# Sparse-attention stacks planned head by head, top-k steps and latent sums moved, in a two-block fp32 transformer kernel

## The chip, the cores and the metric

The kernel runs on one core of one Trainium2 chip. The metric is the device time of one execution in microseconds (us), lower is better. PE is the matrix engine (TensorE), DVE the vector engine, ACT the scalar engine, POOL GpSimd, and SP the engine whose queue issues all DMAs here.

## The reference

`first_block` (pooling, gated linear attention, forgetting attention, gated feed-forward) is followed by `second_block`, both on a [512, 1024] fp32 activation. The change touches the second block only:

```
h = rmsnorm(x, norm_g)
q_lat, c_kv, k_rope, z_a, q_b, k_b, v_b, z_b, q_idx, k_idx, w_idx, gate_a, gate_b = split(h @ w_in)
q  = rmsnorm(q_lat, g_q_lat) @ w_uq          # 8 heads of 64 + 32 (rope)
kv = rmsnorm(c_kv, g_kv_lat) @ w_ukv         # latent ("mla") attention
y_a = mla_attention(q, kv, rope(k_rope)) * silu(z_a)          # 8 heads, chunk-causal
score = sum over 8 index heads of relu(q_idx . k_idx) * w_idx  # per query block of 128
idx = top_k(score, 128)                       # keys a query may see
y_b = dsa_attention(q_b, k_b, v_b, idx, rel_bias) * silu(z_b)  # 8 heads of 64
x = x + (sigmoid(gate_a) * (y_a @ w_o_a) + sigmoid(gate_b) * (y_b @ w_o_b)) @ w_out
```

## The kernel before

Activations lie transposed, [feature, token], so a product is a chain of 128x128 weight tiles against 128x512 activations. Each fp32 product is done as three matmuls on rounded halves (WH with the high and low half of the activation, WL with the high half: L1346, L1347, L1348). Weights come as 164 units of eight tiles through three buffers (WS); ACT rounds a unit (WH, L1516), POOL or DVE subtracts (WL, L2090 or L1765), and SP loads the unit three further on when the subtraction is done.

A planner in Python writes one list of steps; each engine then runs its own instructions of that list in that order, each waiting on semaphores. So an instruction that waits holds all that stand behind it on its engine. A product of n tiles is planned in pieces of two tiles (six matmuls). `weave(main, side, per)` plans one turn of the main generator (index scores, or attention, two turns for each block of 128 queries of a head) and then `per` pieces of the side generator. At every piece but the last of a product, `go_behind` adds `now["per"]` to a due count and plans as many steps from the lists `first` (DSA stacks) and then `behind` (top-k) as are due.

The second block, in order:

- Index scores: for query blocks i = 3, 2, 1 and eight heads, one matmul (L1496), a relu on ACT (L1710), and a weighted sum on DVE into `score` (L2007, L2010). Four banks and four relu buffers rotate. When a block's scores are summed, its cut (L2014) and 16 top-k steps follow, each a MAX8 (L2019) and a MATCH_REPLACE8 (L2021) on 128 x 128(i+1) values, then the mask (L2026). The side work is `latents`: the products ckv0, ckv1, ql0, ql1, ql2 and za0. Each output goes through DVE (L2030), a square on ACT (L1524), a sum on POOL (L2135, L2138), and is halved by ACT (L1714) and DVE (L2035). The column sums (L1377, L1383) of the squares of ckv feed `norm_kv` on ACT (L1718 to L1726: Ln, Ln, Exp, Exp with two table loads), those of ql feed `norm_q` (L1729, L1732). `mla_v` and the first `mla_products` follow. Outputs of query products (a_q) leave their bank on DVE (L2046).
- Attention: four pairs of latent heads, then four pairs of DSA heads, woven with `mla_side`: the other latent products, the DSA products qb, kb and v, the z gates, and the output gates and products. Four a_q, a_k buffers rotate.
- A DSA head needs a stack in one of three slots: the high and low half of q in `b_s1`, the high half of k twice in `b_m1`, the low half twice in `b_m2`. ACT rounds q and k (L1692, L1694), DVE subtracts (L1979, L1982), and SP copies each k half to the other 64 partitions (L1274, L1279). The logits are L1455 and L1456. A head's slot is free again when its last logits are done. `st` (b_st) holds a pair's products until its stacks are made. Before, the stacks of a pair are planned as five steps; a pair's attention begins (`dsa_ready`) when all five are planned, the masks are planned, and the pair's gate zb is there.
- RT holds the rotation table, read for the rope of the keys and by `norm_q` (L2039).

Of the kernel before, what the change touches and what calls it, by code (L numbers as in the profile page):

```python
# [9 lines left out]
F32R = mybir.dt.float32r  # L10
# [152 lines left out]
def build(nc, wall, xT, vecs, wa, wp, relb, cf, cph, coh, cb, scratch, outT):  # L163
    plan = []
    ctx = ExitStack()
    with ctx:
# [104 lines left out]
        LKL = sub("LKL", [128, 2, T], F32R, 32)  # L271
        sq0, sq1 = (at(f"sq{i}_late", [128, T], F32R, o) for i, o in enumerate(sq_at))
        b_s1 = [sub("b_s10", [128, T], F32R, 16), sub("b_s11", [128, T], F32R, 22), sub("b_s12", [128, T], F32R, 56)]
        b_m1 = [sub("b_m10", [128, T], F32R, 18), sq1, sub("b_m12", [128, T], F32R, 64)]
        b_m2 = [sub("b_m20", [128, T], F32R, 20), sub("b_m21", [128, T], F32R, 2), sq0]
        b_st = [[sqb[0], sub("b_st0", [128, T], F32, 2)], [sub("b_st1", [128, T], F32, 58), sub("b_st2", [128, T], F32, 52)],
                [sub("b_st3", [128, T], F32, 58), sub("b_st4", [128, T], F32, 66)]]
# [630 lines left out]
        do("keys", t1=t1, free1=free1, t2=t2, free2=free2)  # L908
        tmp_ring.give(m1, rope("end"))
        tmp_ring.give(m2, rope("end"))  # L910
        now["per"] = 0.6

        def index_scores():
            for i in (3, 2, 1):
# [29 lines left out]
        def latents():  # L944
            for c in range(2):
                yield from product(f"ckv{c}", "w_in_2", 0, cols(P_CKV + 128 * c), "h3", NK,
                                   lat_out(c, "lk", f"ckv{c}", acc[1]))
            bias_rows()
            do("row_out")
            for c in range(3):  # L950
                yield from product(f"ql{c}", "w_in_2", 0, cols(P_QL + 128 * c), "h3", NK,
                                   lat_out(c, "lq", f"ql{c}", acc[0]))
                do("copy_rows", heads=((0, 1, 2), (3, 4, 5), (6, 7))[c])
                if c == 0:
                    i1, b1 = column_sums("lk", acc[1], total_g(("lk", 1)))
                    i2, b2 = token_sums("lkt", [acc[1]], total_g(("lk", 1)))
                    do("norm_kv", b1=b1, b2=b2)
                    t_ring.give(i1, norm_a("lk ln"))
                    t_ring.give(i2, norm_a("lkt ln"))
            for n, _ in enumerate(z_products("za", P_ZA, 0)):  # L960
                if n == 2:
                    i, b = column_sums("lq", acc[0], total_g(("lq", 2)))
                    do("norm_q", b=b)
                    t_ring.give(i, norm_a("lq ln"))
                yield
# [82 lines left out]
        slot_ring, bt_ring = Ring([0, 1, 2]), Ring(b_t)  # L1048
        pc_ring = Ring(Pc)
        pc_ring.free = [None, None, idx_v((1, 7))]  # L1050
        dsa_in, slot_of = {}, {}
        bias_at = {}

        def dsa_v():
# [12 lines left out]

        def dsa_stack(p):

            for n in range(5):  # L1070
                hl, what = n // 2, "qk"[n % 2]
                if n < 4:
                    if what == "q":
                        while not slot_ring.ready() or "uq7" not in known:
                            yield "not yet"
                        i, _, free = slot_ring.take()
                        slot_of[2 * p + hl] = i, free
                    i, free = slot_of[2 * p + hl]
                    do("bstack_high", p=p, hl=hl, what=what, i=i, free=free)
                if n > 0:  # L1080
                    hl, what = (n - 1) // 2, "qk"[(n - 1) % 2]
                    i, free = slot_of[2 * p + hl]
                    do("bstack_low", p=p, hl=hl, what=what, i=i, free=free)
                if n == 4:
                    dsa_in[p] = True
                yield

        def dsa_products(p):
            while (p == 1 and ("logits", ("mla", 5, 3)) not in known) or (p == 2 and ("logits", ("mla", 7, 3)) not in known) \
                    or (p >= 2 and p - 1 not in dsa_in):  # L1090
                go_behind()
                yield "not yet"
            free = [[total_g(("lq", 2)), idx_p((1, 7))], [logits(("mla", 5, 3))], [logits(("mla", 7, 3))], []][p]
# [6 lines left out]

        def dsa_pair(p):
            z_i, z = gates[f"zb{p}"]

            def begun(hl, i, u):
                hd = 2 * p + hl
                if i == 3:
                    bt_ring.give(bias_at[hd][0], row_max(u))
                    slot_ring.give(slot_of[hd][0], logits(u))
                if i == 0:
                    dsa_bias(hd + 1)  # L1110
            return {"a": "dsa", "p_no": p, "qk": [slot_of[2 * p][0], slot_of[2 * p + 1][0]], "begun": begun, "to": "yb",
                    "to_n": p, "z": z, "z_ring": z_ring, "z_i": z_i, "bias": bias_at}

        def gate(m, kind, col, g):
# [24 lines left out]
        def mla_side():  # L1139
# [2 lines left out]
            yield from mla_products(2)  # L1142
            yield from gate_a(0)
            yield from mla_products(3)
            yield from dsa_v()
            dsa_bias(0)
            yield from z_products("zb", P_ZB, 0)
            yield from dsa_products(1)
            yield from gated_ya(0)
            yield from z_products("zb", P_ZB, 1)  # L1150
            yield from dsa_products(2)
            yield from z_products("zb", P_ZB, 2)
            yield from gate_a(1)
            yield from dsa_products(3)
            yield from gated_ya(1)
            yield from z_products("zb", P_ZB, 3)
            for m in range(2, 8):
                yield from gate_a(m)
                yield from gated_ya(m)

        def dsa_ready(p):
            if p not in dsa_in or "masks" not in known:
                step_behind()
            return p in dsa_in and "masks" in known and f"zb{p}" in gates

        now["per"] = 1.4
        side = mla_side()
        for _ in range(3):
            next(side)
# [1120 lines left out]
```

## Time and profile before

| | |
|---|---|
| median of 3 runs | 1110.09 us (1109.54 to 1114.36) |
| the profiled execution, its own time | 1110.54 us |
| its span, first to last instruction | 1108.8 us |
| PE busy | 1052.4 us (95%) |
| DVE, ACT, POOL busy | 625.8 (56%), 474.4 (43%), 261.7 (24%) us |
| mean granted TensorE clock | 0.984 |

Busy time is the time in which an engine runs an instruction. "PEclk" is the TensorE clock that was granted, as a share of the full 2.4 GHz. In lists of instructions a bracket at the end gives how long the engine stood idle ahead of the instruction and what released it. Where a wait has several conditions, the one named is an inference.

### The profile page before, as it was taken

What the parts mean: (1) busy time and instruction counts of PE and PEld (TensorE: products, weight loads), DVE (VectorE), ACT (ScalarE), POOL (GpSimd) and SP (SyncE); (2) the same over time, 40 slices, a digit from 0 to 9 for tenths busy, and PEclk for the clock granted to TensorE, in tenths of its full rate; (3) what the DMA queues carried; (4) which work ended last, traced back from release to release, by engine and by line L of the source; (5) the groups of instructions that cost most, each with busy time, mean ns of one, the idle gap of its engine ahead of it and who ended that gap; (6) DMA issues with size and microseconds to landing.
All of it is one profiled execution on the core that took longest, in us unless ns stands there. A gap on an engine that the chain in (4) does not pass through costs nothing.

```text
span 1108.8 us, 13432 instructions
## 1 busy us (share of the span) xinstructions
PE 1052.4 (95%) x5124; PEld 843.6 (76%) x5132; DVE 625.8 (56%) x1038; ACT 474.4 (43%) x819; POOL 261.7 (24%) x158
## 2 busy tenths in 40 slices
PE   7799899899999999999999998899999999999995
PEld 5597687677888888888888776677887766788883
DVE  6755667756445432444445366898656664325554
ACT  6634345545323221222243456455655453423232
POOL 0581332222110100001113333222322322421101
PEclk9899999999999999999999999999999999999998
DMA  7031132212322232232323326211322333222221
GB/s 291 9 125 42 58 97 89 67 57 79 111 96 95 95 114 95 77 109 85 111 95 96 107 69 201 77 58 58 96 67 91 93 98 90 77 95 93 98 95 76
DMA packets 33919, 103.37 MB, mean 93 GB/s; under 512 B 4576, under 2 KB 6000, under 8 KB 33856
## 3 DMA queue, kind: packets, MB, share of 16 engines
q1 hardware_dynamic: 33856, 102.51, 28.3%
q8 instruction: 41, 0.67, 0.3%
q14 instruction: 22, 0.18, 0.1%
HBM read 94.40 MB, written 4.74 MB: 89 GB/s over the span
## 4 chain that ended last, share of the span: by engine, by line
PE 75%; DVE 13%; ACT 5%; issue 4%; SPq 2%; DMA 1%; DVEq 0%; ACTq 0%; POOL 0%; POOLq 0%
PE bank L1346 21%; PE bank L1348 20%; PE bank L1347 20%; PE bank L1478 2%; PE bank L1469 2%; PE bank L1358 2%; PE bank L1360 1%; PE bank L1359 1%; DVE score L2010 1%; DVE m L2019 1%; DVE score L2021 1%; ACT WH L1516 1%; DVE f_s L1809 1%; PE bank L1450 1%; DVE acc L1779 1%
## 5 line engine op out<-in xcount | busy, mean ns | idle before, releaser
L1346 PE MATMUL bank<-HH,WH 128*128 128x512 f32 x808 | 330.3, 409 | 15.9 <-DVE WL L1765 8.1
L1348 PE MATMUL bank<-HH,WL 128*128 128x512 f32 x808 | 318.3, 394 | 0.0
L1347 PE MATMUL bank<-HL,WH 128*128 128x512 f32 x808 | 317.6, 393 | 0.0
L2090 POOL TENSOR_TENSOR WL<-WS,WH 128x1024 fp32r<-128x1024 f32 x64 | 154.9, 2421 | 360.1 <-ACT WH L1516 359.7
L1516 ACT ACTIVATE WH<-WS 128x1024 fp32r<-128x1024 f32 x164 | 170.7, 1047 | 56.0 <-PE bank L1348 40.6
L1346 PEld LDWEIGHTS bank<-HH,WH 128*128 128x128 f32 x808 | 154.3, 191 | 52.8 <-DVE WL L1765 8.1
L1348 PEld LDWEIGHTS bank<-HH,WL 128*128 128x128 f32 x808 | 153.2, 190 | 33.5
L1347 PEld LDWEIGHTS bank<-HL,WH 128*128 128x128 f32 x808 | 153.9, 191 | 29.5 <-issue 1.0
L1765 DVE TENSOR_TENSOR WL<-WS,WH 128x1024 fp32r<-128x1024 f32 x100 | 132.7, 1333 | 29.5 <-ACT WH L1516 29.5
L2143 POOL TENSOR_TENSOR fa<-fa,fg 128x512 f32<-128x512 f32 x22 | 28.3, 1286 | 273.4 <-DVE fa L1956 273.4
L1346 PE MATMUL bank<-GH,WH 128*128 128x512 f32 x176 | 68.5, 389 | 0.0
L1347 PE MATMUL bank<-GL,WH 128*128 128x512 f32 x176 | 68.5, 389 | 0.0
L1348 PE MATMUL bank<-GH,WL 128*128 128x512 f32 x176 | 68.5, 389 | 0.0
L1936 DVE TENSOR_TENSOR X<-X,bank 128x512 f32<-128x512 f32 x40 | 27.4, 685 | 65.0 <-PE bank L1348 64.9
L1659 ACT ACTIVATE GH<-fa 128x512 fp32r<-128x512 f32 x22 | 13.9, 632 | 114.3 <-POOL fa L2143 114.3
L1524 ACT ACTIVATE sq<-X 128x512 f32<-128x512 f32 x31 | 19.5, 628 | 71.6 <-DVE X L1936 71.5
L1358 PE MATMUL bank<-WH,HH 128*128 128x256 f32 x160 | 47.8, 299 | 2.0 <-ACT f_v L1542 2.0
L1627 ACT ACTIVATE PT<-bank 128x128 f32<-128x128 f32 (+1 forms) x96 | 41.2, 429 | 17.9 <-PE bank L1469 17.6
L1360 PE MATMUL bank<-WH,HL 128*128 128x256 f32 x160 | 45.7, 286 | 0.0
L1359 PE MATMUL bank<-WL,HH 128*128 128x256 f32 x160 | 45.7, 285 | 0.0
L1958 DVE TENSOR_TENSOR GL<-fa,GH 128x512 fp32r<-128x512 f32 x22 | 15.2, 693 | 46.8 <-ACT GH L1659 46.8
L1655 ACT ACTIVATE fs<-fg 128x512 f32<-128x512 f32 x22 | 13.9, 632 | 59.6 <-DVE fg L1947 59.6
(336 smaller groups left out, 1748.5 us busy)
## 6 DMA issues: line engine op xcount, KB each, us to landing
WS<-wall SPq DMA_DIRECT2D x164, 512.0 KB, 3.4
scratch<-rows SPq DMA_DIRECT2D x8, 320.0 KB, 5.4
X<-xT SPq DMA_DIRECT2D x8, 256.0 KB, 6.9
b_t<-scratch SPq DMA_DIRECT2D x8, 256.0 KB, 3.8
b_m<-b_m SPq DMA_DIRECT2D x11, 128.0 KB, 4.3
outT<-X SPq DMA_DIRECT2D x5, 256.0 KB, 2.3
f_s<-f_s SPq DMA_DIRECT2D x8, 128.0 KB
f_m<-f_m SPq DMA_DIRECT2D x8, 128.0 KB
```

The costliest lines, as they stand in the source:

```text
L1346: e.matmul(b[:, :], wh, xh[:, at_k, :], start=k == 0, stop=False)
L1347: e.matmul(b[:, :], wh, xl[:, at_k, :], start=False, stop=False)
L1348: m = e.matmul(b[:, :], wl, xh[:, at_k, :], start=False, stop=k == n - 1)
L1358: e.matmul(b[:, 0:256], xh[:, k, cs], wh, start=k == 0, stop=False)
L1359: e.matmul(b[:, 0:256], xh[:, k, cs], wl, start=False, stop=False)
L1360: m = e.matmul(b[:, 0:256], xl[:, k, cs], wh, start=False, stop=k == NK - 1)
L1516: e.activation(WH[:, u % NW, :], WS[:, u % NST, :], ACT.Copy).then_inc(*w_hi.tick(u))
L1627: e.activation(dst, s["b"][:, 0:128 * i + 128].rearrange("p (a n) -> p a n", n=128), ACT.Copy).then_inc(*moved.tick(s["u"]))
L1765: e.tensor_tensor(WL[:, u % NW, :], WS[:, u % NST, :], f32(WH[:, u % NW, :]), ALU.subtract).then_inc(*w_low_v.tick(u))
L1936: e.tensor_tensor(X[:, m, :], X[:, m, :], s["b"][:, :], ALU.add).then_inc(*out_v.tick(s["name"]))
L2090: e.tensor_tensor(WL[:, u % NW, :], WS[:, u % NST, :], f32(WH[:, u % NW, :]), ALU.subtract).then_inc(*tick(w_low_g, u))
L2143: e.tensor_tensor(a[:, :], a[:, :], fg[jj % 3][:, :], ALU.mult).then_inc(*tick(gate_up, jj))
```

## The change

Five edits, all in the planner; the instructions of each engine stay the same in kind and number, and their order changes.

1. `b_m12`, the k high half of slot 2, moves from the place at 64 KB (which a latent head's a_q buffer shares) to the memory of RT.
2. Top-k steps: `per` 0.6 becomes 0.4 in the index scores, and 1.4 becomes 1.45 in attention.
3. The column and token sums of the ckv squares, with norm_kv, move from behind ql0 to behind ql1.
4. A DSA stack is planned for each head by itself, three steps each, and a pair may begin when its first head's stack is planned; the second head's is asked for at the first head's last query block.
5. `mla_side` has another order: gate_a(1), dsa_products(1) and zb0 go ahead of dsa_v, zb1 ahead of gated_ya(0), gated_ya(1) ahead of dsa_products(3).

```diff
-        b_m1 = [sub("b_m10", [128, T], F32R, 18), sq1, sub("b_m12", [128, T], F32R, 64)]
+        b_m1 = [sub("b_m10", [128, T], F32R, 18), sq1, at("b_m12", [128, T], F32R, RT_at)]
...
-        now["per"] = 0.6
+        now["per"] = 0.4
...
-                if c == 0:
+                if c == 1:
                     i1, b1 = column_sums("lk", acc[1], total_g(("lk", 1)))
                     i2, b2 = token_sums("lkt", [acc[1]], total_g(("lk", 1)))
                     do("norm_kv", b1=b1, b2=b2)
...
         def dsa_stack(p):
-            for n in range(5):
-                hl, what = n // 2, "qk"[n % 2]
-                if n < 4:
-                    if what == "q":
-                        while not slot_ring.ready() or "uq7" not in known:
-                            yield "not yet"
-                        i, _, free = slot_ring.take()
-                        slot_of[2 * p + hl] = i, free
-                    i, free = slot_of[2 * p + hl]
-                    do("bstack_high", p=p, hl=hl, what=what, i=i, free=free)
-                if n > 0:
-                    hl, what = (n - 1) // 2, "qk"[(n - 1) % 2]
-                    i, free = slot_of[2 * p + hl]
-                    do("bstack_low", p=p, hl=hl, what=what, i=i, free=free)
-                if n == 4:
-                    dsa_in[p] = True
-                yield
+            for hl in range(2):
+                hd = 2 * p + hl
+                while not slot_ring.ready() or "uq7" not in known:
+                    yield "not yet"
+                i, _, free = slot_ring.take()
+                for n in range(3):
+                    if n < 2:
+                        do("bstack_high", p=p, hl=hl, what="qk"[n], i=i, free=free)
+                    if n > 0:
+                        do("bstack_low", p=p, hl=hl, what="qk"[n - 1], i=i, free=free)
+                    if n == 2:
+                        slot_of[hd] = i
+                    yield
...
-                    or (p >= 2 and p - 1 not in dsa_in):
+                    or (p >= 2 and 2 * p - 1 not in slot_of):
...
         def dsa_pair(p):
             z_i, z = gates[f"zb{p}"]
+            qk = [slot_of[2 * p]]
...
-                    slot_ring.give(slot_of[hd][0], logits(u))
+                    slot_ring.give(slot_of[hd], logits(u))
+                    if hl == 0:
+                        while hd + 1 not in slot_of:
+                            step_behind()
+                        qk.append(slot_of[hd + 1])
...
             yield from mla_products(3)
+            dsa_bias(0)
+            yield from gate_a(1)
+            yield from dsa_products(1)
+            yield from z_products("zb", P_ZB, 0)
             yield from dsa_v()
-            dsa_bias(0)
-            yield from z_products("zb", P_ZB, 0)
-            yield from dsa_products(1)
+            yield from z_products("zb", P_ZB, 1)
             yield from gated_ya(0)
-            yield from z_products("zb", P_ZB, 1)
             yield from dsa_products(2)
             yield from z_products("zb", P_ZB, 2)
-            yield from gate_a(1)
+            yield from gated_ya(1)
             yield from dsa_products(3)
-            yield from gated_ya(1)
             yield from z_products("zb", P_ZB, 3)
...
         def dsa_ready(p):
-            if p not in dsa_in or "masks" not in known:
+            if 2 * p not in slot_of or "masks" not in known:
                 step_behind()
-            return p in dsa_in and "masks" in known and f"zb{p}" in gates
-
-        now["per"] = 1.4
+            return 2 * p in slot_of and "masks" in known and f"zb{p}" in gates
+
+        now["per"] = 1.45
```

## Rows read from the trace of the kernel before

**Rows 1.** The page, busy us, share of the span and instructions.
```profile
PE 1052.4 (95%) x5124; PEld 843.6 (76%) x5132; DVE 625.8 (56%) x1038; ACT 474.4 (43%) x819; POOL 261.7 (24%) x158
```

**Rows 2.** Windows: PE, PEld, DVE, ACT, POOL busy (count), granted clock, DMA share, GB/s.
```profile
500.00:600.00 100.00, 100.00 (x443) 82.84 (x442) 48.68 (x53) 33.71 (x44) 18.43 (x15) 1.00 0.29 95
...
660.00:716.00 56.00, 46.11 (x211) 36.60 (x210) 43.03 (x57) 30.29 (x51) 20.39 (x10) 0.93 0.45 145
716.00:755.00 39.00, 37.93 (x178) 27.94 (x177) 34.17 (x84) 18.58 (x46) 9.58 (x4) 0.96 0.17 54
...
885.00:930.00 45.00, 40.34 (x196) 30.86 (x197) 28.53 (x76) 20.53 (x47) 12.14 (x6) 0.96 0.38 109
```

**Rows 3.** PE's waits from 660 to the end: us in total, times, longest.
```profile
PE bank L1377 <- POOL acc L2138: 4.4, 1, 4.4
PE bank L1346 <- DVE a_q L2046: 4.3, 2, 3.1
```

**Rows 4.** Timeline of PE, logits of heads 4, 6: start, us, [idle, releaser].
```profile
890.11 0.30 PE L1455 MATMUL bank<-sq_late,b_s 128*128 128x128 f32 x1 [1.99 <-DVE sq_late L1982]
...
923.35 0.30 PE L1455 MATMUL bank<-b_m,b_s 128*128 128x128 f32 x1 [2.48 <-issue]
```

**Rows 5.** Timeline of PE, index scores and latents.
```profile
681.20 0.34 PE L1496 MATMUL bank<-i_kk,i_qq 96*128 96x384 f32 x1
...
688.85 2.08 PE L1377 MATMUL bank<-acc,ones 128*128 128x512 f32 x2 [4.36 <-POOL acc L2138]
...
713.95 0.50 PE L1346 MATMUL bank<-LQH,WH 128*128 128x512 f32 x1 [3.07 <-DVE a_q L2046]
```

**Rows 6.** Windows of 8 us around three of PE's waits.
```profile
688.00:696.00 8.00, 7.15 (x23) 5.38 (x23) 7.77 (x10) 6.73 (x10) 3.42 (x2) 0.57 0.20 75
712.00:720.00 8.00, 6.05 (x22) 4.83 (x23) 6.92 (x17) 0.86 (x3) 0.00 (x0) 0.79 0.20 66
920.00:928.00 8.00, 5.52 (x21) 4.18 (x20) 2.40 (x9) 2.56 (x5) 2.43 (x1) 0.79 0.63 178
```

**Rows 7.** Timeline of ACT around norm_kv and behind ql1.
```profile
666.88 1.28 ACT L1718 ACT_TABLE_LOAD   x1
668.18 0.69 ACT L1718 ACTIVATE RK<-bank,eps 128x512 f32<-128x512 f32 x1
...
671.25 1.06 ACT L1516 ACTIVATE WH<-WS 128x1024 fp32r<-128x1024 f32 x1 [0.19 <-DMA WS<-wall]
...
679.37 1.05 ACT L1516 ACTIVATE WH<-WS 128x1024 fp32r<-128x1024 f32 x1
```

**Rows 8.** Timeline of DVE, two score lines.
```profile
681.11 2.37 DVE L2007 TENSOR_SCALAR score<-i_t,wi 128x384 f32<-128x384 f32 x1
...
709.09 2.42 DVE L2010 SCALAR_TENSOR_TENSOR score<-i_t,wi,score 128x256 f32<-128x256 f32 x1
```

**Rows 9.** Timeline of POOL, the subtraction beside the first of them.
```profile
680.56 2.70 POOL L2090 TENSOR_TENSOR WL<-WS,WH 128x1024 fp32r<-128x1024 f32 x1 [0.77 <-ACT WH L1516]
```

**Rows 10.** Timeline of DVE, one top-k step on 512 columns.
```profile
711.43 0.68 DVE L2019 MAX8 m<-score 128x8 f32<-128x512 f32 x1
...
712.23 0.68 DVE L2021 MATCH_REPLACE8 score<-m,score 128x512 f32<-128x512 f32 x1
```

**Rows 11.** Timeline of DVE, outputs of kb2 and kb3, low halves of k.
```profile
875.07 0.69 DVE L1782 SCALAR_TENSOR_TENSOR b_st<-bank,Rb 128x512 f32<-128x512 f32 x1 [1.94 <-PE bank L1348]
...
880.89 0.67 DVE L1982 TENSOR_TENSOR b_m<-b_st,sq_late 64x512 fp32r<-64x512 f32 x1
...
909.32 0.68 DVE L1782 SCALAR_TENSOR_TENSOR b_st<-bank,Rb 128x512 f32<-128x512 f32 x1
...
916.00 1.98 DVE L1982 TENSOR_TENSOR b_m<-b_st,b_m 64x512 fp32r<-64x512 f32 x1
```

**Rows 12.** Timeline of SP's queue, copy of head 4's low half of k.
```profile
885.50 0.47 SPq L1279 DMA_DIRECT2D b_m<-b_m  x1
```

**Rows 13.** The tile b_m, time from issue to landing of its copies.
```profile
DMA to landing us min/median/max: 2.2/4.3/4.9
```

More of the change, by code:

```diff
@@ L1050, in build @@
         pc_ring.free = [None, None, idx_v((1, 7))]
-        dsa_in, slot_of = {}, {}
+        slot_of = {}
         bias_at = {}
@@ L1107, in begun @@
                     bt_ring.give(bias_at[hd][0], row_max(u))
-                    slot_ring.give(slot_of[hd][0], logits(u))
+                    slot_ring.give(slot_of[hd], logits(u))
[3 more added lines that the diff above has]
+                        qk.append(slot_of[hd + 1])
                 if i == 0:
                     dsa_bias(hd + 1)
-            return {"a": "dsa", "p_no": p, "qk": [slot_of[2 * p][0], slot_of[2 * p + 1][0]], "begun": begun, "to": "yb",
+            return {"a": "dsa", "p_no": p, "qk": qk, "begun": begun, "to": "yb",
                     "to_n": p, "z": z, "z_ring": z_ring, "z_i": z_i, "bias": bias_at}
```

## The prediction

> **What bounds the kernel now.** First the busy times of the page [rows 1]: the matrix engine (PE) is busy for 95% of the span and no other engine passes 56%, so only time in which PE stands still, or runs at its lower clock, can be won or lost by a change that adds no matmul. The long feed-forward stretch [rows 2] shows the undisturbed rate: 443 matmuls in 100 us, 0.226 us each. Then the same view for the stretches of the second block: PE misses 9.9 us of the 56 between 660 and 716 (latents and index scores) and 4.7 of the 45 between 885 and 930 (DSA attention); between 716 and 755 it misses 1.1 [rows 2]. The list of PE's waits names them [rows 3]: 4.4 us for the sum of squares of the query latents and 4.3 for two query outputs (a_q); 2.0 and 2.5 at two DSA logits (L1455) stand in [rows 4]. The clock column adds what follows a wait [rows 5, 6]: in the 8 us around the wait that ends at 688.85 the granted clock is 0.57 (8 times 0.43, 3.4 us lost), around the one that ends at 713.95 it is 0.79 (1.7), and around the one that ends at 923.35 [rows 4] 0.79 again (1.7); 0.50 of it is the lower of the two levels, 1.2 of 2.4 GHz. So 13.2 us of waits and 6.8 us of low clock are all there is to win; no rate of top-k steps gives more.
>
> **Part 1: the latent sums and norm_kv go from behind ql0 to behind ql1.** Nothing is added: 1 column sum and 4 token sums on PE, six instructions on ACT. What counts is where ACT meets them. In the trace they run from 666.88 on, two table loads of 1.28 us among them, and the weight copy behind them starts at 671.25 after 0.19 us of idling for its DMA [rows 7]: 4.2 us of work, all of it done before the copy could start. The weight load came late because the index and key copies stood ahead of it on SP's queue, and the change moves none of these. So ahead of ql1 the 4.2 us are hidden, and taking them away lets no later relu start sooner. Behind ql1 they fall between the relu of (3,7) and the weight copy that now starts at 679.37 [rows 7], where ACT has no slack: copy and the relus of (2,0) to (2,2) go from 679.4 to 683.6. The engine (DVE) that sums the scores then starts (2,0) at 685.1 instead of 681.1, and is held by POOL's subtraction as it is now: POOL 680.56 for 2.70 us, the DVE line 681.11 for 2.37 [rows 8, 9]; both move by 4.2. The latent of ql2, queued behind (2,0), (2,1), (2,2), comes 4.2 us later, less the one top-k step (1.44, below) that no longer stands ahead of it: +2.8. PE waits on it through square, POOL sum and column sum: 688.85 becomes 691.6 [rows 5]. A new wait comes ahead of it: the index matmul (2,4) needs the bank that the relu of (2,0) empties, so PE, which starts it at 681.20 now [rows 5], stands until 685.1.
>
> On the price of the table loads the trace and the Trainium skill differ. In [rows 7] the load takes 1.28 us and the Ln behind it begins at once. The Trainium skill (ScalarE: Activation LUTs, What ACT_TABLE_LOAD costs) gives about 2.66 us for a switch, its drain included; by that the moved group would take 6.9 us and this part would cost 2.8 us more. The measured group decides.
>
> **Part 2: top-k steps, 0.6 to 0.4 for each piece, then 1.4 to 1.45.** A piece is a pair of k tiles (six matmuls, 1.36 us); a step is planned at a piece that is not the last of its product. Counting through the seven such pieces between the first mask cut and the end of the scores gives 4 steps now and 2 after, and the two that go are the ones ahead of the last two a_q outputs. A step on 512 columns is a MAX8 and a MATCH_REPLACE8 of 0.68 us each with a short load between them, 1.44 us [rows 10]. PE stood 1.2 and 3.07 us for these outputs [rows 3, 5]. With everything 2.95 us later by part 1 and two steps (2.9) fewer, the last output would come when it does now; but the score ahead of it, held for 2.42 us [rows 8] by POOL, then comes before POOL's next subtraction, whose weight copy follows PE. PE gets on at 712.6 instead of 713.95: -1.35 (0 if the score is held all the same). Of the 1.7 us at low clock behind that wait I take half as won, since the new waits of 3.9 us (part 1) and near 2.9 (the first output that mla_v needs, zb at L1782) can leave a slow phase of their own: -0.85. The two steps are paid back later: 44 steps become 46, and by piece 22 of latent attention 1.1 steps more have run than now (1.5 us). DVE is busy 34.2 of 39 us there and PE has 1.1 us idle [rows 2], so most is hidden: +0.5, bounds 0 and 1.4. If the whole delay of part 1 stayed and the cover were gone, parts 1 and 2 would cost +4.2; at best they give -3.0. Sum: -1.7.
>
> **Part 3: order of the side work, stacks by head, b_m12 in RT.** The memory only removes a clash: head 2's stack can be written while latent head 7 still uses the old place. RT is last read by norm_q, long before. No instruction is added; a stack has three steps a head (six a pair, five now). dsa_products(1) and gate_a(1) go ahead of dsa_v, so heads 2 and 3 are ready early, but nothing waits for them now: PE's only waits at L1455 are at heads 4 and 6 [rows 4]. So heads 4 and 6 decide. A pair starts when its zb gate is known and its first stack is planned. I count pieces at 0.9 and 0.85 for each half unit of attention, with the not-ready turns (the count gives the one turn seen ahead of pair 0). From the last piece of kb2 to the first logit of head 4: 7 pieces and 4 units now, 5 pieces and 2 units after, because dsa_products(2) moves behind zb1 and gated_ya(0) and pair 2 starts on zb2. From kb3 to head 6: 7 pieces now, 5 after, since gated_ya(1) goes ahead of dsa_products(3). In time: kb2 leaves at 875.07 and PE reaches head 4 at 888.1, 13.0 us; kb3 at 909.32, head 6 at 920.9, 11.6 us [rows 4, 11]. Less two pieces (2.7 us), and for head 4 two units (some 1.6): PE arrives 8.7 and 8.9 us after the product.
>
> The stack needs longer than that. The low half of k ends 6.5 us after kb2 and 8.7 after kb3 [rows 11]; its copy for head 4 goes out 3.9 us after that, at 885.50, because SP's queue stood at a weight load for a split on POOL [rows 12]; the one for head 6 goes at once; landing takes 4.3 us in the median, 2.2 to 4.9 [rows 13]. PE gets on at 890.11 and 923.35 [rows 4]: 15.0 and 14.0 us in all. I take 12.0 for head 4 (6.5, a short hold of 1.2, 4.3) and 13.0 for head 6 (nearest its own rows). Waits: 3.3 and 4.1, and 1.7 of low clock behind each, 10.8 in all, against 6.2 now: +4.6. Bounds: ready after 10.5 in both, no low clock, 3.4 in all, -2.8; ready after 15.0 and 14.0 as now, 6.3 and 5.1 plus 3.4 and one more slow slice, +9.6. No edit of this part that moves product order costs PE anything by itself: the pieces are the same, and the weight tiles move in multiples of eight, so unit ends stay.
>
> The landing time is the other place where the Trainium skill and the rows differ. The row says 4.3 us for 128 KB while weight loads of 512 KB share the queues. The Trainium skill (DMA: Bandwidth & Descriptors, Anatomy of one DMA) makes it about 2.0 us plus the bytes at 436 GB/s, 2.3 us. By that each stack would be ready 2 us sooner and the sum would fall by about 4.
>
> **The sum.** -1.7 + 4.6 = +2.9 on the profiled execution's 1110.54, which lies 0.4 above the median of 1110.09: 1113.
>
> **Rivals.** (a) The likeliest, above: 1113, own range 1108 to 1118. (b) Faster: copies of the stack land in 2.2 us [rows 13], SP is not held, and the half planned earlier comes through ACT and DVE in 4.5 us, because heads 4 and 6 no longer share the queues with a second head of the same stack. Then the stack is ready within 7 us, both DSA waits and their low clock (6.2) go, and with -3.0 from the latents the time is 1101. For it: the order is hq, hk, lk without the next head's copies between; against it: no row shows a stack ready in under 10.5. It decides from a readiness of 8.8 us. (c) Slower: the stack keeps its 14 to 15 us, PE stands over 5 us at head 4 and head 6, and the latent chain keeps +1: 1121. For it: the only two stacks that PE waited for took that long. (d) No change: PE's shift in the latents is taken up by the waits that follow, and slack at DSA stays about what it is: 1110. This is also the case in which the plan by head does nothing, since the zb gates already hold the pairs back. A fifth case lies inside (a): the copies land in the 2.2 us of [rows 13] but nothing else speeds up; the sum falls by 4 to 1109, and I give that 0.08 of the 0.40. The Trainium skill's DMA rule, above, would lead there, its table rule to 1116.
>
> **How the numbers follow.** (a) 0.40, (b) 0.24, (c) 0.22, (d) 0.14. About 0.5% (5.5 us, so 1104.6 and 1115.6) is what a measurement of this kernel tells from no change. (a) lies within it for 0.31 and above for 0.09; (b) is below but for 0.01; (c) above but for 0.03; (d) within. Faster 0.23, same 0.49, slower 0.28. The range 1102 to 1120 leaves out half of (b) and a third of (c).
>
> **What would show it.** Right: norm_kv on ACT near 679 to 684 and a PE wait of about 4 us at an index matmul near 681; the column sum of the query latents near 691.6; a_q waits under 2 us in all; two more MAX8 after 716; waits of 3 to 4 us at L1455 for heads 4 and 6, with a slice of low clock behind. Wrong: a PE wait near 684 that shrinks (then ACT had slack that I did not see); no wait at L1455 at all; a new long wait elsewhere, for a mask at head 0 or a bias row, of which I expect none.

## The result and the profile after

The changed kernel takes 1126.95 us in the median (1125.62 to 1128.81, 5 runs), the one before 1110.86 in the runs beside it (1109.54 to 1114.36): a ratio of 1.0135, 95% interval 1.0118 to 1.0152. It is slower by some 16 us; the forecast was 1113, and its range ended at 1120. All ratios leave out single runs far above the others, which the medians keep: 1385.34 us in `e6_sums_back` (its median is 1120.51 without it), 5170.13 in `e8_both_heads` (1113.34) and 2911.86 in the kernel before beside them.

The page of the changed kernel, busy times (as in [rows 1]); its span is 1125.1 us:

```profile
PE 1059.0 (94%) x5132; PEld 847.5 (75%) x5132; DVE 629.3 (56%) x1038; ACT 474.7 (42%) x819; POOL 261.7 (23%) x158
```

Totals hardly move, so I cut both spans at four points: the first index matmul, the first latent logits, the first DSA logits, the last product of DSA attention with v. For each stage stand its length, the time in which PE is not busy, and the time at low clock (1 less the granted clock, times the length; ahead of the index scores summed over windows of 8 us):

| stage, us | before: length, idle, low clock | after: length, idle, low clock | change |
|---|---|---|---|
| up to the index scores | 659.26, 27.59, 6.8 | 662.35, 28.53, 8.6 | +3.1 |
| index scores and latents | 57.55, 9.89, 4.03 | 56.32, 9.39, 3.38 | -1.2 |
| latent attention | 115.14, 1.20, 1.15 | 119.67, 6.98, 0 | +4.5 |
| DSA attention | 127.14, 4.82, 1.27 | 137.13, 8.41, 6.86 | +10.0 |
| rest | 149.71, 12.88, 4.49 | 149.63, 12.81, 4.49 | -0.1 |

The sum is +16.3: 9.7 of it PE standing still, 5.6 its lower clock. The clock is read to two digits, so a figure for low clock can be off by half a hundredth of its stage's length, 0.6 us in the DSA stage; summed over windows of 4 us it is 1.7 before and 6.8 after there. Three stages hold a loss, and the instructions of the first are the same in both kernels.

PE's waits of the changed kernel from 655 to 980 us (total, times, longest), as in [rows 3]:

```profile
PE bank L1456 <- issue: 7.4, 2, 4.4
PE bank L1497 <- ACT i_t L1711: 4.4, 2, 3.7
PE bank L1470 <- ACT Pc L1620: 3.9, 4, 2.0
PE bank L1371 <- DVE zb L1783: 3.5, 1, 3.5
PE bank L1378 <- POOL acc L2139: 1.5, 1, 1.5
PE bank L1347 <- DVE acc L2051: 1.4, 1, 1.4
PE bank L1347 <- DVE b_st L1783: 1.1, 1, 1.1
```

Lines are one higher than before (L1456 is L1455). The 4.4 for the column sum has become 1.5 and the 4.3 for a_q is gone, but an index matmul (4.4, before 0.5), a zb bank (3.5, before 0.4), turned blocks of latent attention (L1470: 3.9, before 1.1), two products there (2.5, before 0.2) and the two DSA logits (7.4, before 4.5) take more than they gave. Their places on PE's timeline, to be read against [rows 4, 5]:

```profile
688.23 0.45 PE L1497 MATMUL bank<-i_kk,i_qq 96*128 96x384 f32 x1 [3.68 <-ACT i_t L1711]
...
694.71 1.12 PE L1378 MATMUL bank<-acc,ones 128*128 128x512 f32 x2 [1.51 <-POOL acc L2139]
...
702.55 0.58 PE L1371 MATMUL bank<-WH,LKH 128*128 128x256 f32 x1 [3.46 <-DVE zb L1783]
...
904.69 0.44 PE L1456 MATMUL bank<-sq_late,b_s 128*128 128x128 f32 x1 [4.43 <-issue]
...
938.43 0.44 PE L1456 MATMUL bank<-b_m,b_s 128*128 128x128 f32 x1 [3.00 <-issue]
```

ACT's timeline, as in [rows 7], shows what makes PE wait at 688.23: norm_kv now stands between the relu of (3,7) and the weight copy.

```profile
674.45 1.06 ACT L1517 ACTIVATE WH<-WS 128x1024 fp32r<-128x1024 f32 x1 [4.49 <-DMA WS<-wall]
...
682.68 1.28 ACT L1719 ACT_TABLE_LOAD   x1
683.98 0.69 ACT L1719 ACTIVATE RK<-bank,eps 128x512 f32<-128x512 f32 x1
...
686.76 1.04 ACT L1517 ACTIVATE WH<-WS 128x1024 fp32r<-128x1024 f32 x1
```

The gap of 4.49 us for a weight load ahead of ql1 is where norm_kv stood: taking it away only let ACT wait longer, and behind ql1 its 4.1 us (682.68 to 686.76) go straight into the chain.

Windows of the changed kernel (columns as in [rows 2]): the first part of latent attention, and 8 us at each of the two DSA waits, as in [rows 6].

```profile
718.67:755.00 36.33, 33.06 (x152) 24.07 (x151) 34.27 (x82) 15.96 (x39) 9.21 (x4) 1.00 0.17 58
...
904.00:912.00 8.00, 7.31 (x27) 6.14 (x27) 3.29 (x12) 2.31 (x7) 0.00 (x0) 0.59 0.16 37
936.00:944.00 8.00, 5.57 (x16) 4.56 (x17) 5.57 (x11) 4.12 (x8) 2.59 (x1) 0.62 0.33 85
```

DVE is busy for 34.27 of 36.33 us where it was 34.17 of 39 [rows 2], and PE now stands for 3.3 of them instead of 1.1. (The two windows hold 152 and 178 matmuls, so they are not quite the same work.) The windows at the waits run at 0.59 and 0.62, 3.3 and 3.0 us lost, where the one at head 6 before lost 1.7 [rows 6].

### The profile page after: what moved, and what is told of

Its sections match the earlier page's. It is cut to its first block, busy times and chain, and to the rows that moved or that the text cites. A ratio compares the mean times of both kernels' runs of the same rounds, so it can differ in the third digit from the quotient of the medians.

```text
span 1125.1 us, 13443 instructions
## 1 busy us (share of the span) xinstructions
PE 1059.0 (94%) x5132; PEld 847.5 (75%) x5132; DVE 629.3 (56%) x1038; ACT 474.7 (42%) x819; POOL 261.7 (23%) x158
## 4 chain that ended last, share of the span: by engine, by line
PE 71%; DVE 14%; ACT 7%; issue 4%; SPq 2%; DMA 1%; DVEq 0%; ACTq 0%; POOL 0%; POOLq 0%
PE bank L1347 20%; PE bank L1349 19%; PE bank L1348 19%; PE bank L1479 2%; PE bank L1470 2%; DVE score L2022 2%; DVE m L2020 2%; ACT WH L1517 1%; PE bank L1359 1%; PE bank L1361 1%; PE bank L1360 1%; DVE f_s L1810 1%; DVE small L1904 1%; DVE acc L1780 1%; DMA WS<-wall 1%
```

## The experiments

Sixteen kernels, in the order in which they ran. "Ratio" is against the kernel before in the same series, with its 95% interval. Stage lengths and waits are of each kernel's profiled execution, of which there is one for each. The kernel before took 1111.5 us in the median beside e1 to e4, 1112.49 beside e5 to e8, 1111.1 beside e9 to e12 and 1110.81 beside e13 to e16. A pair's cover is the time from the last output of its DSA products (kb2 for head 4, kb3 for head 6) to the moment at which PE comes to the head's first logits.

**The parts one at a time.** `e1_order`: the new place of b_m12 and the new order of `mla_side` (the diff's part 5).

> The kernel before with the new order of the side work and b_m12 in RT; stacks by pair, rates and sums as before. Theory A (the order takes two pieces of cover from the stacks of heads 4 and 6, and puts outputs that go over DVE where the value products stood): the waits at L1455 for the two heads grow from 4.5 to 7 us or more with the low clock behind them, and PE idles more between 755 and 830: 1119 to 1123. Rival B (the plan by head, not the order, makes the stacks late): the waits at L1455 stay at 4.5 us and the time within 3 us of the kernel before.

1120.79 us, ratio 1.0073 (1.0049 to 1.0097). DSA attention takes 136.50 us, 9.4 more than before, and its waits at L1455 are 6.2 with 4.5 at head 4. kb2 leaves at 886.32 and the first logits start at 899.66 after 4.49 us of waiting: PE came 8.9 us behind it. The time is theory A's, the waits stay below its 7 us. The waits in the index scores and latents are as before.

`e2_heads`: the place of b_m12 and the stacks by head (part 4).

> The kernel before with stacks planned by head and b_m12 in RT, order of the side work as before. Theory A: the zb gates hold the pairs back anyway and the low half of a first head's k is planned at the same piece, so nothing moves: within 2 us of the kernel before. Rival B: waits at L1455 of 7 us or more and a time 6 us or more above.

1121.25 us, ratio 1.0087 (1.0058 to 1.0117), DSA attention 134.49 us. This falls on the wrong side of my expectation: planning by head does change when PE comes. PE's waits and the first logits of head 4 in this kernel:

```profile
PE bank L1456 <- issue: 9.1, 3, 5.7
```
```profile
894.72 0.45 PE L1456 MATMUL bank<-sq_late,b_s 128*128 128x128 f32 x1 [5.70 <-issue]
```

kb2 leaves the bank at 879.75, so PE came 9.3 us behind it (894.72 less 5.70), not 13.0 as before.

`e3_sums`: only the sums of part 3.

```diff
-                if c == 0:
+                if c == 1:
```

> The kernel before with the latent sums and norm_kv behind ql1, nothing else. As in the prediction: ACT has no slack there, an index matmul waits some 4 us, the query latents' column sum comes near 693 (a top-k step stands ahead of the latent here), and all stays late up to 716: +3 to +5, 1113 to 1115. Rival: the two a_q waits take the delay up, within 1 us.

1118.27 us, ratio 1.0056 (1.0037 to 1.0076): more than the 1113 to 1115 expected. The stage of the index scores takes 62.74 us, 5.2 more; the index wait of 3.7 us and zb's 1.6 come, the column sum's falls from 4.4 to 1.9, a_q's 4.2 stay, since here the two top-k steps stay ahead of them.

`e4_rates`: only 0.4 and 1.45.

> The kernel before with the rates 0.4 and 1.45 alone. Theory A (two steps fewer ahead of the last a_q outputs, cover for them in attention): -2 to 0. Rival C (DVE has no room between 716 and 830, so the two steps and the denser rate show as PE idle there): +2 to +6, with PE waiting for shares (L1469) and outputs on DVE.

1112.1 us, ratio 1.0005 (0.999 to 1.0019). The a_q waits go, the index stage takes 51.85 us, 5.7 fewer; latent attention takes 118.98, 3.8 more, with PE idle for 4.77 instead of 1.20. This lies between my two theories: both the gain and rival C's loss are there. So the rates only move a loss. The losses of the four singles add up to 2.2%, the whole change costs 1.35%: the parts are not independent. (`e1_order` and `e2_heads` both carry the new place of b_m12. So does `e8_both_heads` below, at no cost clear of the spread of its runs; the place is not what costs.)

**Which rate, and what each part costs in company.** `e5_index_rate`: 0.4 alone.

```diff
-        now["per"] = 0.6
+        now["per"] = 0.4
```

> The kernel before with only the first rate changed (0.6 to 0.4 top-k steps for each piece ahead of the scores' end); the 1.4 of latent attention stays. The run with both rates gained some 5.7 us between the index products and latent attention and lost 3.8 us in latent attention, where VectorE had 98 us of 119 to do. Theory A (the loss comes from the 1.45): the gain stays at 4 to 6 us and the loss is under 1.5, so 1107 to 1108. Theory B (the loss comes from the steps that are left over, whatever the rate is): 1110 to 1112, as with both rates.

1110.6 us, ratio 0.9985 (0.9973 to 0.9997). The index stage gains the same 5.5 us, latent attention loses 2.4 (idle 4.25) and DSA attention 2.7, with a new 1.4 us wait for a mask (nmask): one of the 48 top-k steps now runs behind the first DSA logits, where in `e4_rates`, with 1.45, all run ahead of them. Nearer theory B: the steps left over cost most of it, the 1.45 the other 1.4 in latent attention.

`e6_sums_back`: the changed kernel with the sums behind ql0 again (`c == 0`).

> The changed kernel with the sums of the key latents and norm_kv put back behind ql0. Alone this step cost +6.8 us on the kernel before. Theory A (it costs the same in any company): 1127 less 6.8, so 1120; the 3.9 us wait at index matmul (2,4) and the one at zb near 702 go. Theory B (the fewer top-k steps of the changed kernel already give the engine that sums the scores its room, so most of the price is gone): 1123 to 1126.

1121.74 us, ratio 1.0078 (1.0051 to 1.0104): the index stage takes 51.25 us instead of 56.32, the other stages after it are those of the changed kernel to 0.3 us. The sums cost 5 us in company too (theory A).

`e7_pair_back`: the changed kernel with stacks by pair.

> The changed kernel with the DSA stacks planned by pair again (five steps, a pair begins when all five are planned); order of the side work, place of b_m12, rates and sums stay changed. Theory A (order and plan by head shorten the same cover, so the second adds little): 1124 to 1127. Theory B (each takes its own share of cover, so that taking one back returns it): 1118 to 1121, with DSA waits at the logits near 5 us instead of 7.4.

1121.14 us, ratio 1.0081 (1.0054 to 1.0107); DSA attention 134.04 instead of 137.13, latent attention 117.82 instead of 119.67. The time is theory B's, by four runs that spread from 1118.16 to 1126.49. The waits do not fall as it said, though (6.4 instead of 7.4), and PE comes to head 4 8.9 us behind kb2 as with the plan by head, to head 6 9.3 behind kb3 instead of 8.4. The low clock in DSA attention is 1.7 us where the changed kernel has 6.8.

`e8_both_heads`: as `e2_heads`, but a pair waits for the plan of both its stacks.

```diff
-            return 2 * p in slot_of and "masks" in known and f"zb{p}" in gates
+            return 2 * p + 1 in slot_of and "masks" in known and f"zb{p}" in gates
```

> The kernel before with stacks by head and the other place of b_m12, but a pair begins only when the stacks of both its heads are planned, as before; the run without that condition took +9.7 us and had waits of 5.7 and 3.2 us at heads 4 and 6. Theory A (by head, the pair begins earlier, and the stack is not there yet): waits fall to those of before (2.0 and 2.5) and the time to 1111 to 1114. Theory B (the stack itself comes later because its steps are in another order): waits stay over 4 us in all beyond those of before and the time stays at 1118 to 1121.

1113.85 us, ratio 1.0008 (0.9993 to 1.0023). One condition takes back nearly the whole loss of the plan by head (0.08% of 0.87 are left, and they are not clear of no change). The waits of this kernel:

```profile
PE bank L1456 <- issue: 4.6, 2, 2.3
```

It is the earlier start of the pair, not the other order of the copies, that makes PE meet an unfinished stack: here PE comes to head 4 12.6 us behind kb2, in `e2_heads` 9.3.

**Which half of the order.** `e9_order_late` (zb1 ahead of gated_ya(0), gated_ya(1) ahead of dsa_products(3)) and `e10_order_early` (gate_a(1), dsa_products(1) and zb0 ahead of dsa_v), both with stacks by pair:

```diff
# e9_order_late: behind mla_products(3)
dsa_v, zb0, dsa_products(1), zb1, gated_ya(0), dsa_products(2), zb2, gate_a(1), gated_ya(1), dsa_products(3), zb3
# e10_order_early
gate_a(1), dsa_products(1), zb0, dsa_v, gated_ya(0), zb1, dsa_products(2), zb2, dsa_products(3), gated_ya(1), zb3
```

> The kernel before with only the late half of the new order: zb1 ahead of gated_ya(0), so that dsa_products(2) comes behind both, and gated_ya(1) ahead of dsa_products(3); b_m12 in the rotation table's memory. The whole new order took +8 to +9 us alone. Theory A (cover is lost because the products of pairs 2 and 3 are planned later): all of it is here, 1118 to 1121, with over 5 us of waits at the DSA logits. Theory B (the early half, dsa_products(1) and gate_a(1) ahead of dsa_v, is what costs): 1110 to 1114.

> The kernel before with only the early half of the new order: gate_a(1) and dsa_products(1) ahead of zb0 and dsa_v; behind them gated_ya(0), zb1, dsa_products(2), zb2, dsa_products(3), gated_ya(1), zb3 in the sequence of before; b_m12 in the rotation table's memory. Theory A (see the run of the late half): at the time of before or a little faster, 1108 to 1113, since gate_a(1) no longer stands between the products of pairs 2 and 3. Theory B (the early half is what costs): 1118 to 1121.

1113.86 us, ratio 1.0033 (1.0019 to 1.0047), and 1116.37 us, 1.004 (1.0025 to 1.0055). Neither theory holds: each half costs some 0.35%, and together they make up the 0.73% of `e1_order`. The late half leaves 4.1 us of waiting at head 6, 1.9 at head 4. The early half takes gate_a(1) from between the products of pairs 2 and 3 and leaves 3.3 us at head 4:

```profile
PE bank L1455 <- DMA b_m<-b_m: 3.3, 1, 3.3
```

`e11_full_both`: the changed kernel with the condition of `e8_both_heads`.

> The changed kernel, but a DSA pair begins only when the stacks of both its heads are planned. On the kernel before with stacks by head this condition took back 7 us of 9.7. Theory A (the early start costs here too, what is left is the order's part): 1119 to 1122, as with stacks by pair. Theory B (with the new order the stacks are planned late in any case, the condition is met at the same piece): 1125 to 1128.

1125.12 us, ratio 1.0124 (1.0106 to 1.0141), theory B in the time. DSA attention falls by 2.7 to 134.41 as with stacks by pair, but latent attention rises by 1.5. Of the 5.8 us that stacks by pair give back in the changed kernel, this condition gives 1.8; 3.4 of the difference lie in latent attention (117.82 against 121.18), hardly any in DSA attention (134.04 against 134.41).

`e12_rate_half`: the kernel before with 0.5 in place of 0.6.

> The kernel before with the first rate at 0.5 instead of 0.6 and 1.4 kept: one top-k step fewer ahead of the last query outputs, not two. With 0.4 the stage of the index scores gained 5.7 us, latent attention lost 2.4 and DSA attention 2.7, and 1.7 was left. Theory A (the loss grows with each step left over, the gain comes mostly from the first step that leaves): half the loss and most of the gain, 1106 to 1109. Theory B (gain and loss both go with the number of steps): 1110 to 1112.

1113.04 us, ratio 1.0011 (0.9997 to 1.0025): no gain, and above both theories. One step fewer gains 2.0 in the index stage (a_q still 3.0) and latent attention loses the same 2.4 as with 0.4. So the loss does not go by the number of steps left over.

**Cover given, not taken.** `e13_more_cover`: the kernel before with gate_a(1) ahead of zb2, so that pair 2 can begin only behind the gate's product. `e14_cover_ga2`: also gate_a(2) ahead of zb3.

```diff
-            yield from z_products("zb", P_ZB, 2)
             yield from gate_a(1)
+            yield from z_products("zb", P_ZB, 2)
             yield from dsa_products(3)
             yield from gated_ya(1)
+            yield from gate_a(2)                      # e14 only; left out of the loop below
             yield from z_products("zb", P_ZB, 3)
```

> The kernel before with gate_a(1) ahead of zb2 in the side work, nothing else: pair 2 begins only when zb2 is known, so the gate's product now lies between kb2 and head 4. Theory A (cover is what decides): the wait of 2.0 us at head 4 goes, the one at head 6 stays or moves, 1107 to 1110. Theory B (a pair that begins later costs as much as the wait that it saves, since the gates' products are then missing elsewhere): 1110 to 1113 with a wait of over 2 us in another place.

> As the run before it, and gate_a(2) ahead of zb3 too, so that head 6 gets the same cover. Theory A: both waits at the DSA logits go (4.5 us) and most of the low clock behind them, 1103 to 1107. Theory B (see the run before it): 1109 to 1113.

1108.9 us, ratio 0.9973 (0.9958 to 0.9987), and 1106.79 us, 0.9954 (0.9937 to 0.9971). Theory A in both. In the first, the wait at head 4 is gone and one of 1.8 is left at head 6, where PE comes 12.9 us behind kb3. In the second, PE reaches both heads without a bracket:

```profile
891.07 0.22 PE L1457 MATMUL bank<-sq_late,b_s 128*128 128x128 f32 x1
...
924.59 0.22 PE L1457 MATMUL bank<-b_m,b_s 128*128 128x128 f32 x1
```

kb2 leaves at 875.47, kb3 at 906.40: a cover of 15.6 and 18.2 us. PE's idle time in DSA attention falls from 4.82 to 0.94 us, and the low clock in it from 1.27 to 0. The stage itself is hardly shorter (126.80 against 127.14), since gate_a(2) now lies in it; what is behind it is 5.5 shorter (144.25 against 149.71).

`e15_full_cover`: the changed kernel with dsa_products(2) and (3) each ahead of the gated product that now precedes it.

```diff
             yield from z_products("zb", P_ZB, 1)
-            yield from gated_ya(0)
             yield from dsa_products(2)
+            yield from gated_ya(0)
             yield from z_products("zb", P_ZB, 2)
-            yield from gated_ya(1)
             yield from dsa_products(3)
+            yield from gated_ya(1)
             yield from z_products("zb", P_ZB, 3)
```

> The changed kernel with two swaps in its side work: dsa_products(2) ahead of gated_ya(0), dsa_products(3) ahead of gated_ya(1); stacks by head, rates and sums stay changed. Theory A (the late products take the cover): DSA attention falls from 137 us to 129 to 132 and the time to 1119 to 1122. Theory B (the plan by head and the crowding of the engines behind PE keep the stacks late): the waits at the logits stay over 5 us and the time at 1125 to 1128.

1120.85 us, ratio 1.0086 (1.0067 to 1.0105). DSA attention 130.08 instead of 137.13, the wait at head 4 gone, 3.4 left at head 6: theory A. Two swaps give 5 to 6 us back with everything else changed. But at head 4 it is not the cover alone. It grows from 8.9 to 11.0 us, and the copy of the low half, which the changed kernel sends out 3.4 us behind the subtraction, goes out at once here, so the stack is ready within these 11.0 us:

```profile
895.69 0.67 DVE L1983 TENSOR_TENSOR b_m<-b_st,sq_late 64x512 fp32r<-64x512 f32 x1
...
896.39 0.47 SPq L1280 DMA_DIRECT2D b_m<-b_m  x1
...
899.27 0.31 PE L1456 MATMUL bank<-sq_late,b_s 128*128 128x128 f32 x1
```

`e16_cover_rate`: `e14_cover_ga2` with the first rate at 0.4.

> The kernel before with both gates moved as in the run with gate_a(2), and the first rate at 0.4. Theory A (the gains add up): 1.7 below the run with the gates alone, 1102 to 1106. Theory B (the two steps left over meet the gates' outputs on VectorE in DSA attention): equal to it or slower.

1104.8 us, ratio 0.9942 (0.9924 to 0.996): the fastest kernel of the study, 6 us below the kernel before in its series; it and `e14_cover_ga2` (whose interval it overlaps) beat both kernels. That the rate adds anything to the gates is not shown, since the intervals overlap.

**Cover, wait and low clock side by side.** From each kernel's profile, in us; the low clock is that of DSA attention, summed over windows of 4 us.

| kernel | head 4: cover, wait | head 6: cover, wait | low clock |
|---|---|---|---|
| before | 13.0, 2.0 | 11.6, 2.5 | 1.7 |
| changed | 8.9, 4.4 | 8.4, 3.0 | 6.8 |
| `e1_order` | 8.9, 4.5 | 9.3, 1.7 | 5.1 |
| `e2_heads` | 9.3, 5.7 | 10.6, 3.2 | 5.1 |
| `e7_pair_back` | 8.9, 4.4 | 9.3, 2.0 | 1.7 |
| `e8_both_heads` | 12.6, 2.3 | 11.6, 2.3 | 3.4 |
| `e9_order_late` | 11.2, 1.9 | 7.8, 4.1 | 1.7 |
| `e10_order_early` | 9.6, 3.3 | 12.3, 0.8 | 3.4 |
| `e12_rate_half` | 13.0, 1.9 | 11.6, 2.6 | 0 |
| `e13_more_cover` | 15.6, 0 | 12.9, 1.8 | 0 |
| `e14_cover_ga2` | 15.6, 0 | 18.2, 0 | 0 |
| `e15_full_cover` | 11.0, 0 | 12.0, 3.4 | 3.4 |

The waits follow the cover and the time at which the stack is ready. The low clock behind them follows less well: the same waits of 2.0 and 2.5 us have 1.7 us of it before and none in `e12_rate_half`, and waits of 6.4 in all have 1.7 in `e7_pair_back`, where 6.2 in `e1_order` have 5.1.

## Why the prediction was wrong, step by step

**Part 1, where the sums meet ACT: right, and worth more than I gave it.** norm_kv on ACT at 682.7 to 686.8 (said: near 679 to 684; this profile runs 3.1 us later from the start), the index wait 3.68 (said 3.9), the column sum's last wait at 694.71, less the 3.1 at the said 691.6, the wait at zb 3.46 (said near 2.9). What the table loads cost is in the rows: 1.28 us each, and the group 4.1 us, not the 6.9 that the Trainium skill (ScalarE: Activation LUTs, What ACT_TABLE_LOAD costs) would make it. The term that was too small is the delay: I let the sums make everything 2.95 us later, and `e6_sums_back` shows that the index stage ends 5.1 us sooner without them (3.7 of PE's idle time and 1.8 of low clock). The two steps alone win 5.7 (`e4_rates`), because with the a_q waits the low clock goes too (1.56 in place of 4.03); my terms come to 5.15 for them (the 2.95 made up, 1.35 and 0.85). In the changed kernel both meet, and the stage gains 1.2 of the 2.2 said.

**Part 2, "most is hidden: +0.5, bounds 0 and 1.4": wrong.** The steps moved as I counted: of the 48, 43 ran behind the first latent logits before and 45 do now. But latent attention takes 4.5 us more. The rates alone make 3.8 of it (`e4_rates`), 2.4 without the 1.45 (`e5_index_rate`), and `e12_rate_half` loses the same 2.4 with one step left over instead of two; part of the 4.5 hangs on the plan by head, since `e7_pair_back` takes 1.9 back. I priced the steps by the number that had run more (1.1 steps, 1.5 us) and put them against DVE's free time. DVE had little (94% busy in the windows above), and results came late (turned blocks, a stack product, a gate's output), each a wait of 1 to 2 us. The place of the steps shows at the wait for the gate's output (acc). In the changed kernel two steps stand between the last two row maxima ahead of that output, and PE waits:

```profile
775.02 0.55 DVE L2020 MAX8 m<-score 128x8 f32<-128x384 f32 x1
...
776.26 0.56 DVE L2020 MAX8 m<-score 128x8 f32<-128x384 f32 x1
...
778.05 0.68 DVE L2051 SCALAR_TENSOR_TENSOR acc<-bank,Rb 128x512 f32<-128x512 f32 x1
```
```profile
778.78 0.50 PE L1347 MATMUL bank<-LQH,WH 128*128 128x512 f32 x1 [1.39 <-DVE acc L2051]
```

In the kernel before one step stands there, and PE has no such wait:

```profile
770.57 0.55 DVE L2019 MAX8 m<-score 128x8 f32<-128x384 f32 x1
...
772.36 0.68 DVE L2050 SCALAR_TENSOR_TENSOR acc<-bank,Rb 128x512 f32<-128x512 f32 x1
```

The same wait of 1.4 us stands in `e4_rates`, `e5_index_rate` and `e12_rate_half`. So what counts is not the sum of DVE's time alone but which output of DVE a step stands ahead of; for the other waits this is argued, not shown.

**Part 3, the cover: right to half a microsecond.** PE reached head 4 8.9 us behind kb2 and head 6 8.4 behind kb3 (said 8.7 and 8.9). The waits were 4.43 and 3.00, 7.4 in all (said 3.3 and 4.1, 7.4 in all): that the total agrees is luck, since each is off by 1.1 and the two errors cancel. The rows of DVE and of SP's queue for kb2's and head 4's low half, and for kb3's and head 6's:

```profile
891.40 0.68 DVE L1783 SCALAR_TENSOR_TENSOR b_st<-bank,Rb 128x512 f32<-128x512 f32 x1
...
896.03 0.68 DVE L1983 TENSOR_TENSOR b_m<-b_st,sq_late 64x512 fp32r<-64x512 f32 x1 [0.58 <-ACT sq_late L1695]
...
927.01 0.69 DVE L1783 SCALAR_TENSOR_TENSOR b_st<-bank,Rb 128x512 f32<-128x512 f32 x1 [2.25 <-PE bank L1349]
...
934.97 0.67 DVE L1983 TENSOR_TENSOR b_m<-b_st,b_m 64x512 fp32r<-64x512 f32 x1
```
```profile
899.69 0.33 SPq L1227 DMA_DIRECT2D WS<-wall  x1
900.06 0.47 SPq L1280 DMA_DIRECT2D b_m<-b_m  x1
```

For head 4 the low half is ready at 896.7, its copy stands 3.4 us behind a weight load on SP's queue (which itself waited 3.2 us for a subtraction on POOL), and lands 4.6 after issue: 13.3 us in all (said 12.0, with a hold of 1.2). Head 6: 11.4 (said 13.0). The copies land in 2.2 to 4.7 us, 4.3 in the median, in this kernel too. The Trainium skill (DMA: Bandwidth & Descriptors, Anatomy of one DMA) gives its fixed part and its rate for DMAs that GpSimd issues, and these are SP's; the 2.3 us that I made of it is an estimate, and it fits the fastest copy here, not the usual one.

**Part 3, the low clock behind the waits: wrong in size.** I gave 1.7 for each, the least that [rows 6] showed, though the same group showed 3.4 behind a 4.4 us wait. The windows at 904 and 936 lose 3.3 and 3.0, and the stage 6.86 where I had 3.4. This and part 2 are the two terms that failed. The table above shows that 1.7 for each was not out of reach (`e7_pair_back` has 1.7 in all behind 4.4 and 2.0), so the waits alone do not set the size; what does was not found, and a second profile of the same kernel was not taken. For DSA attention I had +4.6 and it was +10.0: waits +2.9, low clock +5.6 (6.86 less 1.27), and 1.5 in small idle gaps and longer matmuls.

**Rival (d), "the plan by head does nothing, since the zb gates already hold the pairs back": wrong.** Before, the pairs follow one another, and the plan of the fifth step, not zb, held pair 2. `e2_heads` cost as much as the order, and `e8_both_heads` gave it back by one condition. My 8.7 us for head 4 came out right all the same, because either edit alone takes the same cover: PE comes 8.9 us behind kb2 with the order (`e1_order`), 9.3 with the plan by head (`e2_heads`), 8.9 with both. With the new order there, the plan by head takes nothing more at head 4 (8.9 in `e7_pair_back` too) and 0.8 at head 6. That is one reason why their losses don't add up.

**The first 660 us.** They are 3.1 us longer in the profile after, with the same instructions: 1.8 of low clock (slices at 120 and 128 us instead of 152) and 0.9 of idle. I count this as spread between executions, which is argued and not shown: `e5_index_rate`, `e14_cover_ga2` and four others take 658.8 to 659.3 as before, the other ten experiments 661.2 to 662.2, among them small changes such as `e12_rate_half`, and the kernel before itself ranges over 4.8 us in its runs. Against it: the four kernels made from the changed one (e6, e7, e11, e15) are all among the ten, and each kernel has one profile only. What sets it was not found. So 13 of the 16 us have a place in the change, and the other 3 have none that is known.

**The sum.** Forecast were -2.2 for the index scores and latents, +0.5 for latent attention and +4.6 for DSA attention, +2.9; measured were -1.2, +4.5 and +10.0, 13.3 in all, and 3.1 more ahead of them. Two slips of the working change little: the upper bound of part 3 comes to +10.3 by its own terms, not +9.6, and a range that ends at 1120 leaves out more than a third of a case (c) that has its middle at 1121.

Rival (c) came nearest in total (1121), for other reasons: the stack did not keep its 14 to 15 us and no wait exceeded 5 us. What stays open: why stacks by pair give 5.8 us back in the changed kernel and the condition alone 1.8 (most of the difference lies in latent attention), and what of the 9 us by which the four singles exceed the whole is not the cover that order and plan by head share.

## What to carry to other kernels

A product whose result must still go through rounding, subtraction and a copy needs a cover that is counted from its output to its first reader: here 11 to 15 us. Work that is due anyway (two gates' products) placed in between won 4 us, while shortening the cover or letting the reader start sooner lost 4 to 10. A PE wait of 3 us or more should be priced with the low clock behind it as a range: here from 1.7 to 3.5 us for each. And background steps on an engine that is busy for over 90% of a stretch were not free here: moved from one stage to another they took back 4 of 6 us.

## What the runs showed that I had not expected

- Low clock behind a wait: 3.3 us behind 4.43 and 3.0 behind 3.00, though PE was busy for 7.31 of the 8 us in the first of these windows, and none behind waits of 1.9 and 2.6 in `e12_rate_half`; with the waits gone (`e14_cover_ga2`) the granted clock is 1.00 over the 126.8 us of DSA attention.
- The place of the low clock in a stretch of the same instructions differs between the profiled executions, and so does its amount, 5.0 to 8.6 us in the first 656 us.
- For head 4 the copy of the low half of k on SP's queue went out 3.3 to 4.0 us behind its subtraction in every profile but one (3.9 before, 3.4 after, 4.0 in `e2_heads`), behind a weight load that waited for POOL. The exception is `e15_full_cover` (0.03 us), which has no wait at head 4: a second cause of the waits, which no run took away by itself.
